# Two state-space heads at a time on TensorE, their decays from one broadcast matmul, and other idle matmuls at the start

## What is computed

```python
def ssd_mixer(u, w_in, conv_w, conv_b, dt_bias, a_log, d_skip, norm_w, w_out):   # 4 groups x 8 heads, head 64, state 128
    z, xbc, dt = jnp.split(u @ w_in, ...)
    xbc = silu(causal_depthwise_conv(xbc, conv_w, conv_b)); xs, bm, cm = jnp.split(xbc, ...)
    dt = softplus(dt + dt_bias); da = dt * -exp(a_log); xdt = xs * dt
    a_cs = jnp.cumsum(da, axis=2)                        # within chunks of 128 tokens
    decay = segsum_exp(da)                               # exp(cs[l] - cs[s]) for s <= l
    cb = einsum('bclgn,bcsgn->bcgls', cm, bm)
    y_diag = einsum('bcgls,bcgrls,bcsgrp->bclgrp', cb, decay, xdt)
    states = einsum('bclgn,bclgr,bclgrp->bcgrpn', bm, exp(a_cs[-1] - a_cs), xdt)
    ...                                                  # prev: the states carried over the chunks
    y_off = einsum('bclgn,bcgrpn,bclgr->bclgrp', cm, prev, exp(a_cs))
    y = (y_diag + y_off + d_skip * xs) * silu(z)
    return rms_norm(y per group, norm_w) @ w_out
```

## Time and profile before

| | |
|---|---|
| runs | 2894.97, 2890.49, 2894.19 us; median 2894.19 |
| span of the profiled execution | 2890.1 us (its time outside the span is not listed) |
| PE busy | 2805.2 us, 97% |
| PEld, DVE, ACT, POOL busy | 79%, 60%, 27%, 60% |
| state-space layer, head loops | 1329 to 1381, 1398 to 1460, 1480 to 1542, 1561 to 1603 us |

### The profile page before, as it was taken

The page is one execution under the profiler, slowest core; times in us unless marked ns, Lnnn a source line. Parts: engine busy times, 40 slices in busy tenths (PEclk is TensorE's granted clock), DMA queues, the critical chain, the costliest instruction groups (busy, mean ns, idle before and its releaser), DMA issues.

```text
span 2890.1 us, 36575 instructions
## 1 busy us (share of the span) xinstructions
PE 2805.2 (97%) x13062; PEld 2291.0 (79%) x13062; DVE 1724.3 (60%) x1974; ACT 790.3 (27%) x1299; POOL 1732.2 (60%) x984
## 2 busy tenths in 40 slices
PE   9899999999899999999998999999999998999999
PEld 6678888888787888877776778888878886788887
DVE  7886666428867665264665558054567776842635
ACT  3433222103443222025555322010222222310202
POOL 5885666665956666654443548666564443666664
PEclk9999999999999999999999999999999999999999
DMA  4102222332012223322111223222231111222221
GB/s 155 59 30 67 98 98 95 103 100 90 23 57 90 94 95 102 103 86 68 65 61 50 72 70 114 95 95 99 76 101 62 63 59 52 88 102 95 97 98 60
DMA packets 66481, 237.40 MB, mean 82 GB/s; under 512 B 7264, under 2 KB 7520, under 8 KB 66336
## 3 DMA queue, kind: packets, MB, share of 16 engines
q1 hardware_dynamic: 65504, 234.00, 24.3%
q10 hardware_dynamic: 832, 1.51, 0.2%
HBM read 233.38 MB, written 2.10 MB: 81 GB/s over the span
## 4 chain that ended last, share of the span: by engine, by line
PE 84%; DVE 7%; DVEq 3%; issue 3%; ACT 1%; POOL 0%; DMA 0%; ACTq 0%; SPq 0%; POOLq 0%
PE ps L476 24%; PE ps L482 24%; PE ps L479 24%; PE ps L1136 2%; DVE qw L2486 1%; PE ps L879 1%; PE ps L639 1%; DVE ps L1785 1%; PE ps L997 1%; PE ps L989 1%; PE ps L992 1%; PE ps L1172 1%; PE ps L882 1%; PE ps L957 0%; DVEq L1904 0%
## 5 line engine op out<-in xcount | busy, mean ns | idle before, releaser
L411 POOL TENSOR_SCALAR w_hi<-w_raw 128x1024 fp32r<-128x1024 f32 x437 | 483.2, 1106 | 1103.6 <-PE ps L476 1019.0
L413 POOL TENSOR_TENSOR w_lo<-w_raw,w_hi 128x1024 fp32r<-128x1024 f32 x437 | 1099.7, 2517 | 36.5
L476 PE MATMUL ps<-x_hi,w_hi 128*128 128x512 f32 x1864 | 745.7, 400 | 24.1 <-DVEq L2160 5.0
L482 PE MATMUL ps<-x_hi,w_lo 128*128 128x512 f32 x1864 | 729.9, 392 | 0.0
L479 PE MATMUL ps<-x_lo,w_hi 128*128 128x512 f32 x1864 | 729.4, 391 | 0.0
L476 PEld LDWEIGHTS ps<-x_hi,w_hi 128*128 128x128 f32 x1864 | 352.1, 189 | 112.4 <-issue 13.7
L479 PEld LDWEIGHTS ps<-x_lo,w_hi 128*128 128x128 f32 x1864 | 352.5, 189 | 74.6 <-issue 4.1
L482 PEld LDWEIGHTS ps<-x_hi,w_lo 128*128 128x128 f32 x1864 | 352.1, 189 | 75.0
L476 PE MATMUL ps<-a_hi,w_hi 128*128 128x512 f32 x512 | 200.0, 391 | 0.0
L482 PE MATMUL ps<-a_hi,w_lo 128*128 128x512 f32 x512 | 199.2, 389 | 0.0
L479 PE MATMUL ps<-a_lo,w_hi 128*128 128x512 f32 x512 | 199.2, 389 | 0.0
(11 more groups left out here) (424 smaller groups left out, 4716.4 us busy)
## 6 DMA issues: line engine op xcount, KB each, us to landing
w_raw<-wts SPq DMA_DIRECT2D x437, 512.0 KB, 3.2
xres<-xT SPq DMA_DIRECT2D x2, 1024.0 KB, 8.6
outT<-xres SPq DMA_DIRECT2D x8, 256.0 KB, 2.1
pf<-pT ACTq DMA_DIRECT2D x2, 512.0 KB, 3.6
prm<-prm SPq DMA_DIRECT2D x1, 452.0 KB, 3.8
lev<-levels ACTq DMA_DIRECT2D x1, 384.0 KB, 4.4
wtmp<-pos SPq DMA_DIRECT2D x1, 128.0 KB, 3.0
ident<-identity SPq DMA_DIRECT2D x1, 64.0 KB, 10.3
```

Source lines behind the costliest of these rows:

```text
L411: nc.gpsimd.tensor_scalar(w_hi[:, s, :], w_raw[:, s, :], 1.0, 0.0, ALU.mult, ALU.add).then_inc(w_rounded[s], 1)
L413: nc.gpsimd.tensor_tensor(w_lo[:, s, :], w_raw[:, s, :], w_hi[:, s, :].bitcast(F32), ALU.subtract).then_inc(w_split[s], 1)
L476: mm = nc.tensor.matmul(out, whi, xhi, start=first, stop=False)
L482: return nc.tensor.matmul(out, wlo, xhi, start=False, stop=last)
```

## The change

Four things. The heads of a pair are issued together (`head_pair`), their matmuls in turn on the two halves of the columns, with four buffers of `seg` and `ctu`. The decay sums' high and low parts lie in one operand `cs_hl`, the low part on partitions 32 to 63, and `ident_r` has ones in both places, so that one matmul broadcasts their sum. The spreads, steps and decays stand in another order: `spread(g, 1)`, `decays(g, 1)` and `decayed(g, 1)` before the loop of heads, and two spreads for each pair. Of the idle matmuls at the start 5 of 8 stay, and shorter ones with fp32r operands of one, two and four times 128 columns come after them.

```diff
-        seg, _ = at("seg", [P, 2, S])
-        ctu, _ = at("ctu", [P, 2, S - P])
-        cs_hi, _ = at("cs_hi", [P, S], F32R)
-        cs_lo, _ = at("cs_lo", [P, S], F32R)
+        seg, _ = at("seg", [P, 4, S])
+        ctu, _ = at("ctu", [P, 4, S - P])
+        cs_hl, _ = at("cs_hl", [P, S], F32R)
...
+            def idle_r(b, n, parts):
+                for i in range(n):
+                    nc.tensor.matmul(ps[b][:, 0:parts * P].rearrange("p (a q) -> p a q", a=parts), ones_r[:, :],
+                                     ones_r[:, :].unsqueeze(1).to_broadcast([P, parts, P]), start=i == 0, stop=i == n - 1)
             pe.wait_ge(acc_free[0], 1)
-            idle(5, 8)
+            idle(5, 5)
+            idle_r(5, 5, 4)
+            idle_r(4, 4, 2)
+            idle_r(5, 4, 1)
+            idle_r(5, 9, 4)
...
-                nc.tensor.matmul(ps[3][:, :], col, cs_hi[:, :], start=True, stop=False)
-                nc.tensor.matmul(ps[3][:, :], col, cs_lo[:, :], start=False, stop=True).then_inc(csb_done, 1)
-            def head(g, r):
...
+                nc.tensor.matmul(ps[3][:, :], col, cs_hl[:, :], start=True, stop=True).then_inc(csb_done, 1)
+            def head_pair(g, p):
+                n, out = GT * g + p, ps[4 + p % 2]
+                pe.wait_ge(m_ready, 2 * n + 2)
+                if p == 0:
+                    pe.wait_ge(xdt_ready, TT * (g + 1))
+                    pe.wait_ge(h_ready, 2 * (g + 1))
+                if n >= 2:
+                    pe.wait_ge(y_read, n - 1)
+                both = [(r, slice((r % 2) * HD, (r % 2 + 1) * HD)) for r in (2 * p, 2 * p + 1)]
                 for tt in range(TT):
+                    c = slice(tt * P, (tt + 1) * P)
+                    for r, rows in both:
+                        mm = nc.tensor.matmul(out[rows, c], xdt[:, tt, r * HD:(r + 1) * HD], seg[:, r % 4, c],
+                                              start=True, stop=tt == 0)
                     if tt:
+                        for r, rows in both:
+                            mm = nc.tensor.matmul(out[rows, c], hst[:, tt - 1, r * HD:(r + 1) * HD],
+                                                  ctu[:, r % 4, (tt - 1) * P:tt * P], start=False, stop=True)
                 mm.then_inc(yh_done, 1)
...
                     steps_of(ahead, some)
+                    if c == 0:
+                        spread(g, 1)
                     if c == 0 and g:
                         norm_sum(g - 1)
...
-                for r in range(GH):
-                    steps_of(ahead, (4 if g else 3) if some else 2)
-                    if r + 1 < GH:
-                        spread(g, r + 1)
-                    steps_of(ahead, (4 if g else 3) if some else 1)
-                    head(g, r)
+                for p in range(GT):
+                    steps_of(ahead, (5 if g else 4) if some else 2)
+                    if p + 1 < GT:
+                        spread(g, 2 * p + 2)
+                    steps_of(ahead, (6 if g else 4) if some else 2)
+                    if p + 1 < GT:
+                        spread(g, 2 * p + 3)
+                    steps_of(ahead, (5 if g else 4) if some else 2)
+                    head_pair(g, p)
...
             def decays(g, r):
-                if k >= 2:
-                    act.wait_ge(yh_done, k - 1)
+                if k >= 4:
+                    act.wait_ge(yh_done, k // 2 - 1)
...
                 AC.activation(hst[:, 0, :], ps[6 + n % 2][:, :], ACT.Copy).then_inc(h1_ready, 1)
                 act.drain().then_inc(misc_free[n % 2], 1)
+                decays(g, 1)
                 if g:
                     norm_root(g - 1)
...
-                    if r + 1 < GH:
+                    if 1 <= r < GH - 1:
                         decays(g, r + 1)
...
-            V.tensor_copy(ident_r[:, :], ident[:, 0:SH])
+            V.tensor_tensor(ident_r[:, :], ident[:, 0:SH], ident[:, SH:2 * SH], ALU.add)
...
-            V.tensor_tensor(cs_lo[:, :], cs[:, :], cs_hi[:, :].bitcast(F32), ALU.subtract).then_inc(small_dve, 1)
+            V.tensor_tensor(cs_hl[SH:2 * SH, :], cs[0:SH, :], cs_hl[0:SH, :].bitcast(F32), ALU.subtract).then_inc(small_dve, 1)
...
+                decayed(g, 1)
                 for r in range(GH):
...
-                    if r + 1 < GH:
+                    if 1 <= r < GH - 1:
                         decayed(g, r + 1)
```

More of the change, by code:

```diff
@@ L255, in program @@
         cb, _ = at("cb", [P, S])
-        seg, _ = at("seg", [P, 2, S])
-        ctu, _ = at("ctu", [P, 2, S - P])
-        cs, _ = at("cs", [P, S])
-        cs_hi, _ = at("cs_hi", [P, S], F32R)
-        cs_lo, _ = at("cs_lo", [P, S], F32R)
-        csT, _ = at("csT", [P, TT, SH])
-        dtT, _ = at("dtT", [P, TT, SH])
+        seg, _ = at("seg", [P, 4, S])
+        ctu, _ = at("ctu", [P, 4, S - P])
+        cs_hl, _ = at("cs_hl", [P, S], F32R)
+        csT, _ = at("csT", [P, TT, SH], F32, o_rope + 640)
+        dtT, _ = at("dtT", [P, TT, SH], F32, o_rope + 1152)
         w_t, _ = at("w_t", [P, TT, SH])
@@ L265, in program @@
         cend, _ = at("cend", [P, TT, SH], F32, o_y + 4 * 2048)
-        ident_r, _ = at("ident_r", [P, SH], F32R)
-        aex, _ = at("aex", [P, 1])
+        cs, _ = at("cs", [P, S], F32, o_y + 5 * 2048)
+        ident_r, _ = at("ident_r", [P, SH], F32R, o_rope + 1664)
+        aex, _ = at("aex", [P, 1], F32, o_rope + 1792)
         tri, _ = at("tri", [P, P], F32, o_onr)
@@ L1433, in decays @@
                 act.wait_ge(csb_done, k + 1)
-                if k >= 2:
-                    act.wait_ge(yh_done, k - 1)
+                if k >= 4:
+                    act.wait_ge(yh_done, k // 2 - 1)
                 for tt in range(TT):
-                    AC.activation(seg[:, r % 2, tt * P:(tt + 1) * P], ps[3][:, tt * P:(tt + 1) * P], ACT.Relu,
+                    AC.activation(seg[:, r % 4, tt * P:(tt + 1) * P], ps[3][:, tt * P:(tt + 1) * P], ACT.Relu,
                                   bias=csT[:, tt, k:k + 1], scale=-1.0)
-                AC.activation(ctu[:, r % 2, :], ps[3][:, P:], ACT.Exp).then_inc(csb_read, 1)
+                AC.activation(ctu[:, r % 4, :], ps[3][:, P:], ACT.Exp).then_inc(csb_read, 1)
                 act.wait_ge(csb_read, k + 1)
-                AC.activation(seg[:, r % 2, :], seg[:, r % 2, :], ACT.Exp, scale=-1.0).then_inc(dec_ready, 1)
+                AC.activation(seg[:, r % 4, :], seg[:, r % 4, :], ACT.Exp, scale=-1.0).then_inc(dec_ready, 1)
             def gated_square(g, p):
@@ L1466, in _ @@
             act.wait_ge(small_dve, 5)
-            AC.activation(cs_hi[:, :], cs[:, :], ACT.Copy).then_inc(small_act, 1)
+            AC.activation(cs_hl[:, :], cs[:, :], ACT.Copy).then_inc(small_act, 1)
             center(0, "x2")
@@ L2207, in pair @@
                 n = GT * g + p
-                dve.wait_ge(yh_done, GH * g + 2 * p + 2)
+                dve.wait_ge(yh_done, n + 1)
                 dve.wait_ge(sz_ready, n + 1)
@@ L2230, in decayed @@
                 dve.wait_ge(dec_ready, k + 1)
-                V.tensor_tensor(seg[:, r % 2, :], seg[:, r % 2, :], cb[:, :], ALU.mult)
-                V.tensor_tensor(ctu[:, r % 2, :], ctu[:, r % 2, :], cT[:, g % 2, P:], ALU.mult).then_inc(m_ready, 1)
+                V.tensor_tensor(seg[:, r % 4, :], seg[:, r % 4, :], cb[:, :], ALU.mult)
+                V.tensor_tensor(ctu[:, r % 4, :], ctu[:, r % 4, :], cT[:, g % 2, P:], ALU.mult).then_inc(m_ready, 1)
             def group_norm(g):
```

10 lines of the change are left out of this document (removed).

## The result

The changed kernel takes 2898.16 us (median of 20 runs) and the kernel before 2893.2 (20 runs): ratio 1.0016, 95% interval 1.0010 to 1.0022. By the ratio it is 4.6 us slower (by the medians 5.0), where 4 us faster was forecast; the range held the time, the direction was wrong.

A forecast was written before the change was run, and what follows sets the result against it. TensorE, with work in 97% of the span, was taken as the bound. 19.0 + 5.6 - 12.6 - 2.8 - 4.5 - 0.8 = 3.9 us faster: forecast 2890 us, range 2876 to 2906.

The forecast's parts named there:

- Heads: TensorE's head pairs in groups 0 to 2: 2.16 us a pair instead of 3.74, 12 pairs, 19.0 us saved.
- Broadcast: Decay broadcast on TensorE: 24 matmuls of 0.23 us go in groups 0 to 2, 5.6 us saved.
- Waits: New TensorE waits for ACT in groups 0 to 2: 12.6 us at spreads, 2.8 at the third state matmul.
- spread 7 in groups 1 and 2: TensorE waits 4.4 us in each group, for ACT's center of x0 and the work up to ctu.
- the third state matmul: Waits for the bank norm_root frees, now behind `decays(g, 1)` on ACT: 1.4 us, twice, 2.8.
- spread 5 in groups 1 and 2: TensorE waits 0.4 us for `decays(4)` behind center B on ACT.
- Clock: Half clock on TensorE behind the waits of 4.4, 4.4 and 2.6: 1.5 us each, 4.5 us; between 0 and 6.
- Group 3: Last group, on a chain, with what follows: 0.8 us slower, between 4 faster and 4 slower.
- Opening: Changed idle matmuls at the kernel's start: 0 us, within 1.5 either way.
- Rival B: Small waits, wholly overlapping halves (pair 1.87 us), no clock lost: 16 us faster, 2878; chance 0.30.
- rival C: Column halves run one behind the other, a pair costs 3.40 us: 14.7 us slower, 2909; chance 0.18.
- D: Forecast plus unwalked waits at group ends or 2 us more cold clock per wait: 2896; chance 0.15.

The follow-up runs named there:

- x3_bcast: Kernel before with only the one-matmul broadcast (`cs_hl`, `ident_r`), order, buffers and heads as before; ratio 0.9979 to the kernel before, 6.1 us faster.
- x4_actfirst: Changed kernel with ACT reordered: next head's decays first, then gated square one iteration later, then center and silus; ratio 0.9904 to the kernel before.
- x5_best: x4_actfirst with `norm_root(g - 1)` ahead of `decays(g, 1)` on ACT and the old opening; ratio 0.9891 to the kernel before.
- x7_lag: Changed kernel with only the gated square one iteration later on ACT, behind the decays; center and silus stay ahead; ratio 0.9939 to the kernel before.
- x9_norm_late: Changed kernel with group_norm on DVE in iteration 3 instead of 1, behind pair 0; ratio 0.9997 to the kernel before.
- x6_fill: Changed kernel with 68 idle broadcast matmuls in place of its five long waits in groups 0 to 2; ratio 0.9989 to the kernel before.
- x2_opening: Kernel before with only the new idle matmuls at the start; ratio 1.0004 to the kernel before, interval 0.9991 to 1.0017.
- x8_late: Changed kernel with spreads, decays and DVE products back in the places of the kernel before; ratio 0.9916 to the kernel before.
- x1_serial: Changed kernel with the heads of a pair one after the other, seven matmuls each, not alternating; ratio 1.0056 to the kernel before.

## Why the prediction was wrong

- **Heads.** Forecast 2.16 us a pair, taken between 1.87 and 3.40; measured 1.87, the high end. Saved in groups 0 to 2: 22.4, not 19.0. Of the two statements of the Trainium skill that stood against each other (TensorE: Matmul & The Clock Gate, Part 3), the trace agrees with the one that column tiles run at the same time, here twice as fast for two of them (the skill: 2.38 for three). It disagrees with the one that weight loads overlap only where the row group differs: these halves share all rows, and 28 records with their loads fit in the time of 14.
- **Broadcast.** 5.6 us forecast, 5.8 measured in x3_bcast.
- **Waits.** Right: spread 7 in groups 1 and 2 (4.4 forecast, 4.11), in group 0 (2.6, 2.92), spread 3 in group 0 (0.4, 0.29), the third state matmul (1.4, 1.2), with the causes named; x4_actfirst, x5_best and x7_lag take them away one by one, all but the 0.29. Wrong: spread 5 in groups 1 and 2. I put it down to center B, 0.4 us; it is 2.73, and the cause is the gated square behind pair 0 behind group_norm (x7_lag and x9_norm_late both bring it to 0.24). I had walked this very chain for group 3 and left it out here. What makes it late are DVE's durations: the product of 0.69 became 2.85 and the four of 4.1 to 4.3 became 5.4, some 3.3 us in all. Without these 3.3 the square would have been done at about 1418.1 (an estimate: 1420.83 + 0.54 - 3.3), ahead of the 1418.9 at which center B could start (its last matmul at 1418.43, plus 0.43), and spread 5 would have waited some 0.2. No run takes the slowdown away alone. The kernel before shows it too: its product at 1346.51 took 2.88 us, and I planned with 0.69. That step is 4.7 us short; with the other waits 0.9 less than forecast, the waits are 19.2 and not 15.4.
- **Clock.** Forecast 1.5 us for each of three waits, 4.5. Five waits had the effect, and behind those of 4.11 it cost more: from 1442.86 to 1447.69 11 matmuls take 4.8 us in place of 2.5, and in group 2 13 take 5.7 in place of 3.0; behind the other three it cost 1.5 to 1.7 each. Read from the starts in this way the five cost 9.9 us, and x6_fill, which fills the waits and changes little else, gets back 9.4. The account of the whole stretch leaves a little more: groups 0 to 2 saved 28.0 and waited 19.2 more, which leaves 8.8 faster; they were 2.3 slower, so 11.1 are to be explained. The remaining 1.2 fits the way in which waits are counted: an idle time is counted from the end of the last matmul, 0.39 behind its start, where the next would have started 0.23 behind it, so each of the eight new waits costs 0.16 more than its figure. This term is the larger of the two errors: 5.4 us for the clock, 6.6 with that edge.
- **Group 3.** Forecast 0.8 slower on a chain with a wait of "nearly 10"; 2.6 slower with 11.19, at a mean clock of 0.90 where it was 0.94. How the 1.8 us between them divide was not tested.
- **Opening.** Forecast 0, within 1.5; x2_opening and the markers show no difference.

Put together, groups 0 to 2 were forecast 4.7 us faster; 3.4 more from the heads, 3.8 less from the waits and 6.6 less from the clock with the edges of the waits make 2.3 slower, as measured. The mechanism of the forecast stands (a saving on TensorE, given back at the spreads by the order of ACT). The steps that failed are two of its costs: the clock, charged at 4.5 us for three waits where five waits cost 9.9, and the wait ahead of spread 5, put at 0.4 where it is 2.7. Both were too small. Rival B was right on the overlap and wrong on the waits; rival C is excluded; D, which named waits that I had not walked or more cold clock per wait, came nearest to the time, and both were there.

What stays open: the profile of the changed kernel carries 3.5 us ahead of group 0 that no other run of the same opening shows, and the slowdown of DVE beside GpSimd was not taken away by itself.

## What to carry to other kernels

When a change makes one engine's stream shorter and also moves its requests earlier, count in steps of that stream when each thing ahead of the answer, on the engine that answers, can be ready: an in-order engine answers only after everything written ahead of it, and a wait on an unrelated producer (here a square for a norm) is passed on. A program at 97% on one engine has no slack for that: 32 us lay in the place of two calls on an engine that is 54% busy in the head loop. Ask also whether the early requests are needed at all: here, with enough other work ahead of each pair, they were not (x8_late). Price a wait with the half clock behind it, which cost here some 10 us on 16.6 us of waiting, and take durations from the crowded rows of a timeline, not from the quiet ones.

## What the runs showed of the hardware

- Float32 matmuls of 64 columns of weights, in turn on the two column halves with all 128 rows, run two at a time: 28 records with their own weight loads in 1.53 us, as 14 before. In x1_serial, one head after the other, only the eight records around the change of half overlap (starts 0.055 apart, else 0.11).
- The length of a wait alone does not say whether half clock (1.2 GHz) follows. In the changed kernel's opening it followed on waits of 1.81, 0.48 and 1.81 us with three matmuls behind each of the first two (starts 0.43 apart from 21.22 to 24.20, and 0.23 apart on either side), and in group 3 on waits of 0.99 and 1.60 (granted clock 0.50 from 1561 to 1567), while the 1.65 at group 3's spread 3 and the 1.19 and 1.20 in groups 1 and 2 had none behind them. Each of the five waits of 2.7 us or more in groups 0 to 2 did. Ahead of a spread that waited 4.11 the clock had fallen during the wait (0.95 from 1439 to 1441, 0.50 from 1441 to 1443), so that only part of the half clock met any work.
- DVE's product of two tiles in SBUF took 2.85 us in place of 0.69 while GpSimd's subtraction ran (1407.05 to 1409.44); it ended 0.55 after that one did, and L2230 at 1433.39 ended 0.54 after the next. With one operand in PSUM, L2227 kept its 0.75 (1432.55). By the Trainium skill (SBUF — State Buffer, SBUF: two separate sides) DVE instructions with two SBUF inputs and GpSimd's share one pair of ports, held by one of them for a whole instruction; the trace agrees.
